# The opening of layer 0 in a two-layer hybrid trunk: another order for loads, sines, angles and rotations

## The chip, the cores and the metric

The kernel runs on one core of a Trainium2 chip. The metric is the device time of one execution in microseconds (us). The core has five instruction queues that run beside each other: TensorE (PE, matmuls and transposes), VectorE (DVE), ScalarE (ACT), GpSimd (POOL) and SyncE (SP, which here only starts DMAs). They meet by semaphores. An instruction that waits holds up everything behind it in its own queue.

## The reference

Two layers over 256 tokens of width 1024, float32. Each layer normalises x, multiplies it with `w_in`, splits the result among three mixers, joins them with `w_out`, and adds a squared-ReLU MLP:

```
h = rms_norm(x, ln1_g[layer])
(a_q, a_ckv, a_kr, i_q, i_k, i_w, b_u, c_q, c_kv, c_gate) = split(h @ w_in[layer])
a_out = dsa_mixer(...)    # an indexer scores keys, top-64 of them are attended to; partial rotary
b_out = s5_mixer(b_u, ...)  # complex diagonal state space, 64 states in 16 groups
c_out = nsa_mixer(c_q, c_kv, c_gate, ...)  # compressed, selected and window branches
x = x + concat(rms_norm(a_out), rms_norm(b_out), rms_norm(c_out)) @ w_out[layer]
x = x + relu(rms_norm(x, ln2_g[layer]) @ w_up[layer])**2 @ w_down[layer]
```

After the second layer x is normalised once more. The rotary angles are `positions * THETA**(-2i/n)`, and the S5 part needs the powers of `exp((lambda_re + i*lambda_im) * exp(log_step))`.

## The kernel before, in words

**Weights in pieces.** All weights go through a ring of four buffers `raw[0..3]` of 128 x 1024 elements. SP loads piece n. ACT rounds it (`hi(n)`, w_hi, line 871). DVE takes the rest of it (`lo(n)`, w_lo, line 1314). PE multiplies in three passes (`mm3`, line 1744): high by high, low by high, high by low. `lo(n)` frees the raw buffer, so it lets SP start piece n+4; PE's last matmul on piece n frees w_hi for `hi(n+4)`. Pieces 0 to 19 are `w_in`, in five column tiles of four pieces each (`TILES`; tiles 0, 2, 3 have 512 columns, tile 1 has 308, tile 4 has 280). Pieces 20 to 31 are `w_out`, the rest `w_up` and `w_down`. The activations are split the same way: `h_parts` (ACT, h_hi, line 864) and `h_rest` (DVE, h_lo, line 1242), from x that PE transposed block by block (`transpose_x`, line 1773; x comes in four column blocks of 256, two blocks of 128 rows of h each).

**The order is written by hand.** Each engine's program is one list; nothing moves at run time. In the opening of layer 0:

- SP (line 496 on) starts `pos_i`, `step_rows` and four small row loads into `vrow_a`, then pieces 0 to 3 (`first_pieces`), then the rows of `vrow_b`, `craw`, the parameters `ukv` and `glw`, then the pieces that wait for `lo`.
- ACT (line 844 on) starts the four x blocks and `braw` (`load_b`). Then it copies the transposed rows (`vectors`), makes h_hi and w_hi in turn, does the S5 sines (`s5_trig(0)`), the rope sines of `ang` and `ang3`, the sums of squares of x (`sums`), the table `ct` (`c_table`), and `hi(4)` on.
- DVE (line 1230 on) does the rope angles (13 small instructions from line 1258 to 1270), clears `tk`, then h_lo and w_lo in turn, `turn()` (which writes the sine and cosine tables from the rope sines), and from `lo(8)` on places other work behind each piece by the table `behind` (line 1599): the six steps `far_...` write `ca`, the six steps `near_...` write `bp`, `index_heads` rotates the indexer's queries and keys, `latent_heads`, `queries` and `keys_s` rotate the others, and behind piece 19 stand `s5_lags`, `s5_sums_read`, `s5_states`, `index_sum`, `s5_states_back`.
- POOL (line 588 on) does `prep(0)` (the S5 angles, which ends in `den_s5`), `prep_powers(0)` (ends in `prep_a`; in the middle it makes `r1` from ACT's sums), `prep_rest(0)` (ends in `prep_b`), starts the compression weights, and `prep_outputs(0)`, which fills `rot` by doubling (`double`, 6 instructions each; ends in `prep_r`) and makes `rkv`.
- PE (line 1736 on): all four x blocks are transposed, then `tile(0)` to `tile(4)`, with other work behind some pieces by the dictionary `after`.

After `tile(4)` come ten units of attention in which PE, DVE, ACT and POOL hand each other scores (line 1638 is the DVE end of it), then `w_out` and the MLP, which are almost all matmuls.

Of the kernel before, what the change touches and what calls it, by code (L numbers as in the profile page):

```python
# [43 lines left out]
CQ = 8  # L44
# [97 lines left out]
def trunk(nc, x_in, positions, ln1_g, w_in, kv_norm_g, w_uk, w_uv, s5_lambda_re, s5_lambda_im,  # L142
# [4 lines left out]
    with ctx:  # L147
# [193 lines left out]
        tk_in = [sig(f"tk_in{i}", 0) for i in range(DEPTH)]  # L341
        ix_roped, a_roped = sig("ix_roped", 1), sig("a_roped", 1)
# [154 lines left out]
        def _(sp):  # L497
            sp.dma_start(pos_i[:], positions.rearrange("o (t p) -> p (o t)", p=PART)).then_inc(pos_loaded.sem, 16)
            sp.dma_start(step_rows, s5_log_step.rearrange("l (j g) -> j l g", g=2)).then_inc(step_row.sem, 16)
            sp.dma_start(vrow_a[0:8], ln1_g.rearrange("l (k p) -> k l p", p=PART)).then_inc(rows_a.sem, 16)  # L500
            sp.dma_start(vrow_a[8:16], s5_lambda_re.rearrange("l (j g) p -> j l (g p)", g=2)).then_inc(rows_a.sem, 16)
            sp.dma_start(vrow_a[16:24], s5_lambda_im.rearrange("l (j g) p -> j l (g p)", g=2)).then_inc(rows_a.sem, 16)
            sp.dma_start(vrow_a[24:32], ln2_g.rearrange("l (k p) -> k l p", p=PART)).then_inc(rows_a.sem, 16)

# [9 lines left out]
            first_pieces(0, lambda q: None)  # L514
# [10 lines left out]
            load_params(sp, 0, params0, ("rows",))  # L525
            for L in range(DEPTH):
# [7 lines left out]
                for c0, w in TILES[1:]:  # L534
                    for q in range(4):
                        piece(n, raw[:, n % RING, 0:2 * w].rearrange("p (k n) -> p k n", k=2),
                              w_l[:, 2 * q:2 * q + 2, c0:c0 + w])
                        n += 1
                wo_l = w_out[L].rearrange("(k p) n -> p k n", p=PART)
                wo_c = w_out[L, D_MODEL - C_HEADS * HD:D_MODEL].rearrange("(g j d) n -> d g j n", g=C_KV, d=HD)  # L540
                for half, _, qs, _ in OUT:
                    for q in qs:
# [9 lines left out]
                        if L == 0 and n == 24:  # L552
                            lags_in(sp, L)
# [34 lines left out]
        def _(pool):  # L588
# [112 lines left out]
            def double(e, n, m):  # L701

                w = [e[:, i, :, n:n + 1].to_broadcast([PART, PAIRS, m]) for i in range(2)]
                return cmul(e[:, 0, :, n + 1:n + 1 + m], e[:, 1, :, n + 1:n + 1 + m], e[:, 0, :, 1:1 + m],
                            e[:, 1, :, 1:1 + m], w[0], w[1],
                            *(t[:, 0:PAIRS * m].rearrange("p (j m) -> p j m", m=m) for t in small))

            def prep_outputs(occ):
# [11 lines left out]
                if occ == 0:  # L720
                    rstd(0, 2, rkv[:], stat[:, 2:4], A_RANK)
# [44 lines left out]
            for L in range(DEPTH):  # L766
# [78 lines left out]
        def _(act):  # L845
# [34 lines left out]
            for b in range(4):  # L880
                cols = slice(b * SEQ, (b + 1) * SEQ)
                act.dma_start(x[:, :, cols], x_in.rearrange("o (t p) d -> p (o t) d", p=PART)[:, :, cols])\
                    .then_inc(x_loaded[b].sem, 16)
            load_b(act, 0, first0)

# [9 lines left out]
            vectors(1, pb[6], 0, 40)  # L895
            act.wait_ge(vec_sb.sem, 1)
            for L in range(DEPTH):
                if L == 0:
                    step_s5.by(act.activation(sp[:, 0, :], lam[2][:, 0], ACT.Exp))
                for n in range(4):  # L900
                    if L == 0:
                        h_parts(L, 0, g1[:, L], (2 * n, 2 * n + 1))
                    hi(L, n)
                    if L == 0 and n == 0:
                        act.wait_ge(lrs_s5.sem, lrs_s5.at(0, 1))
                        mag_s5.by(act.activation(sp[:, 1, :], sp[:, 21, :], ACT.Exp))
                    if L:
                        h_parts(L, 0, g1[:, L], (2 * n, 2 * n + 1))
# [13 lines left out]
                if L == 0:  # L922
                    s5_trig(0)
# [3 lines left out]
                    sums(0, 0, sq_sum.by)  # L927
                    c_table(0, 1)
                for n in range(4, 6):
                    hi(L, n)  # L930
# [31 lines left out]
                act.wait_ge(ix_ps.sem, ix_ps.at(L, 1))  # L962
                step(act.activation(iqT, pb[3][:, 0:SEQ], ACT.Copy), False)
                ix_sb.by(act.activation(ikT, pb[3][:, SEQ:2 * SEQ], ACT.Copy))
# [266 lines left out]
        def _(dve):  # L1231
# [14 lines left out]
            for t, v in ((half_neg, -0.5), (cmask, 0.0), (mask8, 1.0), (mhalf, 1.0), (mquart, 1.0),  # L1246
# [9 lines left out]
            dve.wait_ge(pos_loaded.sem, 16)  # L1256
            dve.wait_ge(freq_set.sem, 1)
            step(dve.tensor_copy(pos_f[:], pos_i[:]))
            nf = HALF + I_HALF
            tt(ang[:], pos_f[:].unsqueeze(2).to_broadcast([PART, TT, nf]),  # L1260
               freq[:].unsqueeze(1).to_broadcast([PART, TT, nf]), ALU.mult)
            ts(ang3[:], ang[:], 1.0 / PI2, MAGIC, ALU.mult, ALU.add)
            ts(ang3[:], ang3[:], -MAGIC, None, ALU.add)
            for c in (C1, C2, C3):
                ts(ang2[:], ang3[:], c, None, ALU.mult)
                tt(ang[:], ang[:], ang2[:], ALU.subtract)
# [1005 lines left out]
```

## Time and profile before

| what | value |
|---|---|
| time, median of 3 runs | 657.12 us (655.36 to 657.30) |
| the profiled execution's own time | 657.18 us |
| its span, first to last instruction | 655.4 us |
| PE busy | 618.9 us, 94% of the span |
| DVE busy | 430.0 us, 66% |
| ACT busy | 361.6 us, 55% |
| POOL busy | 234.6 us, 36% |
| chain that ended last | PE 73%, DVE 15%, ACT 5%, issue 3%, POOL 2%, DMA 1% |
| DMA | 102.79 MB, mean 157 GB/s |

The span is what the trace covers; 1.8 us of the time lie around it. "Chain" is the list of work followed back from the last instruction, at each step to what released it: where it runs through one engine, that engine sets the time there. "Idle before" in a row is how long the engine stood still ahead of an instruction, and what ended it. The matmul rows overlap, so the time that one takes from the next is the distance of their starts.

### The profile page before, as it was taken

Reading aid. Unit: us, or ns where it says so; the run is one execution under the profiler, and the core shown is the slowest. Engines: PE = TensorE matmul, PEld = TensorE weight load, DVE = VectorE, ACT = ScalarE, POOL = GpSimd, SP = SyncE. Lnnn points to the kernel's source line nnn. Section 1 sums busy time; section 2 is a strip of 40 time slices with the busy share of each in tenths; the row PEclk is TensorE's granted clock in tenths of the full one; section 3 lists DMA queues with packets and bytes.
Section 4 is the critical chain, followed back from the end, with each engine's and each line's share of the span. In section 5 each row is a group of like instructions: output and inputs, shape, how many; then the busy total and the mean of one; then the engine's idle time right before and its main releaser. Section 6 shows DMA issues by size and latency. Waiting matters only on the chain.

```text
span 655.4 us, 11268 instructions
## 1 busy us (share of the span) xinstructions
PE 618.9 (94%) x4268; PEld 533.2 (81%) x4268; DVE 430.0 (66%) x796; ACT 361.6 (55%) x674; POOL 234.6 (36%) x407
## 2 busy tenths in 40 slices
PE   5999988998999999999999999799899999999995
PEld 4868865688998899889878787568798899899984
DVE  7599898476655696774575877846755545554553
ACT  5756588735546434443456657984545544444451
POOL 6899258515045999910004304771000000000001
PEclk9999998999999999999999999999899999999998
DMA  9584604156854557366638640314466566657631
GB/s 266 168 235 121 140 2 114 33 155 202 258 186 151 185 164 254 128 226 193 190 83 262 124 129 2 82 65 128 134 216 196 167 200 190 188 166 217 192 98 65
DMA packets 55440, 102.79 MB, mean 157 GB/s; under 512 B 12713, under 2 KB 18906, under 8 KB 55354
## 3 DMA queue, kind: packets, MB, share of 16 engines
q1 hardware_dynamic: 48986, 96.04, 48.2%
q0 software_dynamic: 1792, 4.07, 2.6%
q10 hardware_dynamic: 4608, 1.97, 1.1%
q8 instruction: 34, 0.56, 0.4%
q14 instruction: 20, 0.16, 0.1%
HBM read 99.69 MB, written 1.31 MB: 154 GB/s over the span
## 4 chain that ended last, share of the span: by engine, by line
PE 73%; DVE 15%; ACT 5%; issue 3%; POOL 2%; DMA 1%; SPq 0%; DVEq 0%; POOLq 0%; ACTq 0%
PE pb L1744 72%; DVE w_lo L1314 5%; DVE x L1242 2%; ACT tab_zone L1114 1%; ACT w_hi L871 1%; DVE dtmp L1235 1%; POOL dtmp L794 1%; DVE sc_zone L1638 1%; ACT ptmp L1127 1%; DMA raw<-in_w_in 1%; DVE dtmp L1514 1%; DVE top L1510 1%; PE pb L1871 1%; PE pb L2135 1%; DVE tab_zone L1235 1%
## 5 line engine op out<-in xcount | busy, mean ns | idle before, releaser
L1314 DVE TENSOR_TENSOR w_lo<-raw,w_hi 128x1024 fp32r<-128x1024 f32 (+2 forms) x176 | 223.6, 1286 | 139.5 <-ACT w_hi L871 138.6
L871 ACT ACTIVATE w_hi<-raw 128x1024 fp32r<-128x1024 f32 (+2 forms) x184 | 187.9, 1028 | 201.3 <-PE pb L1744 178.5
L1744 PE MATMUL pb<-h_hi,w_hi 128*128 128x256 f32 x512 | 146.1, 285 | 2.5 <-DVE h_lo L1242 1.8
L1744 PE MATMUL pb<-h_hi,w_lo 128*128 128x256 f32 x512 | 145.6, 284 | 0.0
L1744 PE MATMUL pb<-h_lo,w_hi 128*128 128x256 f32 x512 | 145.5, 284 | 0.0
L1744 PEld LDWEIGHTS pb<-h_hi,w_hi 128*128 128x128 f32 x512 | 98.9, 193 | 4.1 <-DVE w_lo L1314 3.0
L1744 PE MATMUL pb<-w_hi,z_hi 128*128 128x512 f32 x256 | 100.0, 390 | 0.4 <-DVE w_lo L1314 0.4
L1744 PE MATMUL pb<-w_hi,z_lo 128*128 128x512 f32 x256 | 99.9, 390 | 0.0
L1744 PE MATMUL pb<-w_lo,z_hi 128*128 128x512 f32 x256 | 99.7, 389 | 0.0
L1744 PEld LDWEIGHTS pb<-h_hi,w_lo 128*128 128x128 f32 x512 | 99.0, 193 | 0.4
L1744 PEld LDWEIGHTS pb<-h_lo,w_hi 128*128 128x128 f32 x512 | 98.9, 193 | 0.0
L1744 PE MATMUL pb<-w_hi,h_hi 128*128 128x512 f32 (+2 forms) x224 | 85.5, 382 | 4.7 <-DVE w_lo L1314 3.8
L1744 PE MATMUL pb<-w_lo,h_hi 128*128 128x512 f32 (+2 forms) x224 | 82.3, 367 | 0.0
L1744 PE MATMUL pb<-w_hi,h_lo 128*128 128x512 f32 (+2 forms) x224 | 82.2, 367 | 0.0
L603 POOL TENSOR_TENSOR tail<-tail 128x1 f32<-128x1 f32 x2 | 0.4, 194 | 178.6 <-ACT proj L1223 178.6
L794 POOL TENSOR_TENSOR dtmp<-tab_zone,cf 128x128 f32<-128x128 f32 x80 | 38.3, 510 | 62.7 <-DVE cf L1654 60.9
L1744 PEld LDWEIGHTS pb<-w_hi,z_hi 128*128 128x128 f32 x256 | 48.1, 188 | 10.5 <-DVE w_lo L1314 0.9
L1744 PEld LDWEIGHTS pb<-w_lo,z_hi 128*128 128x128 f32 x256 | 48.1, 188 | 10.1
L1744 PEld LDWEIGHTS pb<-w_hi,z_lo 128*128 128x128 f32 x256 | 48.1, 188 | 9.4
L1744 PEld LDWEIGHTS pb<-w_hi,h_hi 128*128 128x128 f32 x224 | 42.6, 190 | 14.4 <-DVE w_lo L1314 6.8
L1744 PEld LDWEIGHTS pb<-w_lo,h_hi 128*128 128x128 f32 x224 | 42.5, 190 | 6.9
L1744 PEld LDWEIGHTS pb<-w_hi,h_lo 128*128 128x128 f32 x224 | 42.7, 191 | 5.9
(309 smaller groups left out, 852.3 us busy)
## 6 DMA issues: line engine op xcount, KB each, us to landing
raw<-in_w_up SPq DMA_DIRECT2D x64, 512.0 KB, 3.7
raw<-in_w_down SPq DMA_DIRECT2D x64, 512.0 KB, 4.2
raw<-in_w_in SPq DMA_DIRECT2D x24, 512.0 KB, 4.9
raw<-in_w_out SPq DMA_DIRECT2D x8, 512.0 KB, 3.7
raw<-in_w_out SPq DMA_DIRECT2D x16, 256.0 KB, 4.1
raw<-in_w_in SPq DMA_DIRECT2D x8, 308.0 KB, 3.2
raw<-in_w_in SPq DMA_DIRECT2D x8, 280.0 KB, 3.0
x<-in_x ACTq DMA_DIRECT2D x4, 256.0 KB, 4.0
```

Of the source, the lines that this page charges most:

```text
L794: w = pool.tensor_tensor(pn[:, i, a:b], ex[:, i, a:b], cf[:, i, t:t + 1].to_broadcast([PART, b - a]), ALU.mult)
L871: hi_made.by(act.activation(w_hi[:, n % RING, 0:width(n)], raw[:, n % RING, 0:width(n)], ACT.Copy))
L1114: w = act.activation(ex[:, i, a:b], sc[:, i, a:b], ACT.Exp, scale=-1.0, bias=nmx[:, i, t:t + 1], accum_out=sm[:, i, t:t + 1])
L1127: w = act.activation(pT[:, 2 * (v % 2) + m, :], pb[2 + m][:, 0:384], ACT.Copy)
L1235: step(dve.tensor_tensor(o, a, b, op), wait)
L1242: return dve.scalar_tensor_tensor(out=o, in0=a, scalar=s, in1=b, op0=op0, op1=op1)
L1314: lo_made.by(dve.tensor_tensor(w_lo[:, n % RING, 0:width(n)], raw[:, n % RING, 0:width(n)], w_hi[:, n % RING, 0:width(n)].bitcast(F32), AL ...
L1510: step(dve.max(top8[:, c:c + 8], isc[:, a:b]), False)
L1514: step(dve.match_replace(isc[:, a:b], top8[:, c:c + 8], isc[:, a:b], -3e38), False)
L1638: w = dve.tensor_tensor_reduce(sc[:, i, a:b], pb[m][:, a:b], mask[:, a:b], -(HD ** -0.5), 3e38, ALU.add, ALU.min, nmx[:, i, t:t + 1])
L1744: return pe.matmul(o, l, r, start=start, stop=stop, skip_group_check=True)
L1871: m = pe.transpose(bank[:, a:a + PART], src[:, t], ident[:])
```

## The change

Only layer 0's opening and its column tiles change (the form of `double` also serves layer 1).

**Loads.** SP no longer starts `pos_i`, `lambda_im` and `ln2_g` ahead of piece 0: the last two go out on ACT's queue behind x's first block, and `pos_i` behind piece 1. `braw` moves from ACT's queue to SP's behind piece 5, and `ukv` and `glw` behind piece 7.

**PE.** Blocks 2 and 3 of x are transposed behind pieces 0 and 1. `index_turned` goes from behind piece 8 to behind piece 10, `index_scores` from behind piece 10 to behind piece 11, `u_transposed` from ahead of piece 12 to behind it.

**ACT.** `hi(0)` stands ahead of the row copy and h_hi; the S5 sines stand between blocks 2 and 3 of h_hi; `hi(4)` stands ahead of the sums, `hi(5)` ahead of `c_table`; the rope sines come after `c_table`. The copy of the turned indexer rows (`index_out`) goes behind `tile_out(1)` and its sums, just ahead of `hi(12)`.

**DVE.** The 13 angle instructions go from the start of the program to behind the last h_lo. The clearing of `tk` goes to POOL, behind `load_c`, with a new semaphore that SP waits for before `lags_in`. `far_re` and `turn()` go behind `lo(7)`. `index_heads` is cut into `index_queries` and `index_keys`, one behind piece 9 and one behind piece 10, and the near and far steps get scratch space of their own.

**POOL.** `double` makes both parts in one instruction where it can, 4 instructions for 6; `rkv` is made behind n = 4 and not behind n = 8.

```diff
+            def load_rows(q):
+                if q == 0:
+                    sp.dma_start(step_rows, ...)
+                    sp.dma_start(vrow_a[0:8], ln1_g...)
+                    sp.dma_start(vrow_a[8:16], s5_lambda_re...)
+                if q == 2:
+                    sp.dma_start(pos_i[:], positions...)
+            first_pieces(0, load_rows)
...
+                        if L == 0 and n == 6:
+                            load_b(sp, 0, first0)
+                        if L == 0 and n == 8:
+                            load_params(sp, 0, params0, ("rows",))
...
+                tt(dst, src, w[0], ALU.mult, False)
+                tt(t, src, w[1], ALU.mult)
+                tt(dst[:, 0], dst[:, 0], t[:, 1], ALU.subtract, False)
+                return pool.tensor_tensor(dst[:, 1], dst[:, 1], t[:, 0], ALU.add)
...
+                    tk_clear.by(pool.memset(tk[:], 0.0))
...
                 if L == 0:
-                    behind = {9: (far_re2, far_re3), 10: (near_re, near_re2), 11: (near_re3, near_im),
-                              12: (near_im2, near_im3), 13: (far_im,), 14: (latent_heads,), 15: (far_im2, far_im3),
-                              16: (queries,), 18: (keys_s,),
+                    behind = {8: (far_re2,), 9: (index_queries,), 10: (index_keys,), 11: (near_re, near_re2),
+                              12: (near_re3, near_im), 13: (near_im2, near_im3), 14: (far_re3, latent_heads),
+                              15: (far_im, far_im2), 16: (queries,), 17: (far_im3,), 18: (keys_s,),
...
+                tile(0, {0: (lambda: transpose_x(0, 0, (2,)),), 1: (lambda: transpose_x(0, 0, (3,)),), 2: (lambda: c_transposed(0),)} if L == 0 else {})
...
-                    tile(2, {0: (index_turned,), 2: (index_scores,)})
-                u_transposed()
+                    tile(2, {2: (index_turned,), 3: (index_scores,)})
```

ACT's queue in the opening, before. `x` is the input, `w_hi<-raw` is hi, `h_hi` comes from x turned into banks pb0 to pb3, `sp<-sp` are S5's exponentials and sines, `ang` the rope sines:

```order
L887 ACTIVATE sp<-half_neg 128x8
L892 ACTIVATE vcol<-pb6 128x2x40
L899 ACTIVATE sp<-vcol 128x8
L864 ACTIVATE h_hi<-pb0,vcol 128x256 x2
L871 ACTIVATE w_hi<-raw 128x1024
L906 ACTIVATE sp<-sp 128x8
L864 ACTIVATE h_hi<-pb1,vcol 128x256 x2
L871 ACTIVATE w_hi<-raw 128x1024
L864 ACTIVATE h_hi<-pb2,vcol 128x256 x2
L871 ACTIVATE w_hi<-raw 128x1024
L864 ACTIVATE h_hi<-pb3,vcol 128x256 x2
L871 ACTIVATE w_hi<-raw 128x1024
```

The same place in the changed kernel, up to the sums of squares:

```order
L882 ACTIVATE w_hi<-raw 128x1024
L904 ACTIVATE vcol<-pb6 128x2x40
L875 ACTIVATE h_hi<-pb0,vcol 128x256 x2
L913 ACTIVATE sp<-vcol 128x8
L875 ACTIVATE h_hi<-pb1,vcol 128x256 x2
L882 ACTIVATE w_hi<-raw 128x1024 x2
L918 ACTIVATE sp<-sp 128x8
L882 ACTIVATE w_hi<-raw 128x1024
L875 ACTIVATE h_hi<-pb2,vcol 128x256 x2
L868 ACT_TABLE_LOAD
L868 ACTIVATE sp<-sp 128x8
L869 ACTIVATE sp<-sp 128x8
```

Piece 0's hi moved ahead of the row copy, of the exponential that POOL waits for, and of the first h_hi; the sines moved ahead of the last pair of h_hi, which is the next row there.

DVE's queue from `far_re` to the end of the indexer's rotation, before. `ca` and `dtmp<-pa,ct` are the far steps, `tab_zone<-pa,bb` is the first near step, `iqr` and `ikr` the indexer's queries and keys:

```order
L1235 TENSOR_TENSOR ca<-pa,ct 128x8x128
L1314 TENSOR_TENSOR w_lo<-raw,w_hi 128x1024
L1454 COPY iqr<-proj 128x256
L1455 COPY ikr<-proj 128x256
L1235 TENSOR_TENSOR dtmp<-proj,ric 128x64
L1235 TENSOR_TENSOR dtmp<-proj,ris 128x8x4 x2
L1235 TENSOR_TENSOR iqr<-dtmp 128x8x8
L1235 TENSOR_TENSOR dtmp<-proj,ric 128x16
L1235 TENSOR_TENSOR dtmp<-proj,ris 128x2x4 x2
L1460 TENSOR_TENSOR ikr<-dtmp 128x8x8
L1239 TENSOR_SCALAR cs<-proj 128x8
L1314 TENSOR_TENSOR w_lo<-raw,w_hi 128x1024
```

The same in the changed kernel, from piece 8 on:

```order
L1347 TENSOR_TENSOR w_lo<-raw,w_hi 128x1024
L1269 TENSOR_TENSOR dtmp<-pa,ct 128x1024
L1347 TENSOR_TENSOR w_lo<-raw,w_hi 128x1024
L1494 COPY iqr<-proj 128x256
L1495 COPY ikr<-proj 128x256
L1269 TENSOR_TENSOR dtmp<-proj,ric 128x64
L1269 TENSOR_TENSOR dtmp<-proj,ris 128x8x4 x2
L1269 TENSOR_TENSOR iqr<-dtmp 128x8x8
L1347 TENSOR_TENSOR w_lo<-raw,w_hi 128x1024
L1269 TENSOR_TENSOR dtmp<-proj,ric 128x16
L1269 TENSOR_TENSOR dtmp<-proj,ris 128x2x4 x2
L1503 TENSOR_TENSOR ikr<-dtmp 128x8x8
```

The rotation stood whole between pieces 8 and 9; now one far step stands there, and the rotation's halves stand behind pieces 9 and 10.

## Rows read from the trace of the kernel before

**Rows 1.** Chain in order of time, 0 to 150 us: start us, us, what.

```profile
3.09 6.17 DMA raw<-in_w_in
9.28 1.07 ACT w_hi L871
10.37 1.24 DVE w_lo L1314
11.65 10.53 PE pb L1744 x36
...
24.32 0.65 DVE w_lo L1314
...
31.49 1.31 DVE w_lo L1314
```

**Rows 2.** Windows, DVE alone: stretch, length, busy (instructions), PEclk, DMA share, GB/s.

```profile
24.30:31.50 7.20, 6.60 (x19) 1.00 0.59 171
31.50:67.20 35.70, 32.83 (x50) 1.00 0.65 184
```

**Rows 3.** Queues, 4.5 to 6 us: packets, MB, share of 16 engines.

```profile
q10 hardware_dynamic: 465, 0.38, 92.3%
q1 hardware_dynamic: 35, 0.01, 2.9%
```

**Rows 4.** Timeline of ACT: start us, us, instruction, idle before.

```profile
7.64 0.24 ACT L892 ACTIVATE vcol<-pb 128x80 f32<-128x80 f32 x1 [1.82 <-PE pb L1757]
...
8.03 0.82 ACT L864 ACTIVATE h_hi<-pb,vcol 128x256 fp32r<-128x256 f32 x2
...
17.45 0.21 ACT L857 ACTIVATE sp<-sp 128x8 f32<-128x8 f32 x1 [0.69 <-POOL sp L641]
...
18.17 1.05 ACT L875 ACTIVATE proj<-x 128x1024 f32<-128x1024 f32 x1
...
22.66 0.89 ACT L914 ACTIVATE ct<-pb 64x128 f32<-64x128 f32 x4 [2.17 <-PE pb L1808]
23.57 2.62 ACT L871 ACTIVATE w_hi<-raw 128x616 fp32r<-128x616 f32 x4
```

**Rows 5.** Timeline of PE, 11 to 23 us.

```profile
16.08 0.39 PE L1744 MATMUL pb<-w_hi,h_lo 128*128 128x512 f32 x1
...
22.02 0.60 PE L1808 MATMUL pb<-ident,craw 128*128 128x128 f32 x4
22.37 0.48 PE L1744 MATMUL pb<-w_hi,h_hi 128*128 128x512 f32 x1
```

**Rows 6.** Timeline of DVE, 4 to 68 us.

```profile
4.23 0.17 DVE L1258 CAST pos_f<-pos_i 128x2 f32<-128x2 int32 x1
...
7.00 0.18 DVE L1270 TENSOR_TENSOR ang<-ang 128x24 f32<-128x24 f32 x1
...
11.52 0.87 DVE L1242 SCALAR_TENSOR_TENSOR h_lo<-pb,vcol,h_hi 128x256 fp32r<-128x256 f32 x2
...
63.75 0.23 DVE L1235 TENSOR_TENSOR dtmp<-proj,rc 128x64 f32<-128x64 f32 x1 [0.20 <-ACT proj L948]
...
65.55 0.74 DVE L1314 TENSOR_TENSOR w_lo<-raw,w_hi 128x560 fp32r<-128x560 f32 x1 [0.94 <-ACT w_hi L871]
67.23 0.39 DVE L1444 COPY ytok<-pb 128x224 f32<-128x224 f32 x1 [0.94 <-PE pb L1744]
```

**Rows 7.** Timeline of POOL: S5's preparation and the doubling.

```profile
8.21 0.21 POOL L628 TENSOR_TENSOR sp<-vcol,sp 128x8 f32<-128x8 f32 x1 [2.46 <-ACT sp L899]
...
43.70 1.06 POOL L603 TENSOR_TENSOR rot<-rot 128x8 f32<-128x8 f32 x1
...
66.53 0.42 POOL L617 TENSOR_TENSOR rot<-rot,yz 128x120 f32<-128x120 f32 x1
```

**Rows 8.** Timeline of PE, 96 to 103 us: one unit's scores, then the next.

```profile
96.44 0.93 PE L1744 MATMUL pb<-u_zone 64*128 64x128 f32 x8
...
101.21 1.52 PE L1744 MATMUL pb<-u_zone 64*128 64x128 f32 x8 [2.23 <-DVE nmx L1638]
```

More of the change, by code:

```diff
@@ L719, in prep_outputs @@
                     step(double(rot, n, n))
-                if occ == 0:
-                    rstd(0, 2, rkv[:], stat[:, 2:4], A_RANK)
+                    if occ == 0 and n == 4:
+                        rstd(0, 2, rkv[:], stat[:, 2:4], A_RANK)
                 prep_r.by(double(rot, 16, 15))
@@ L926, in _ @@
                     act.activation(ang[:], ang3[:], ACT.Sin).then_inc(trig_rope.sem, 1)
[L927 to L930, printed above, removed]
+                else:
+                    for n in range(4, 6):
+                        hi(L, n)
                 if L:
@@ L961, in _, with index_out @@
                         input_rows(act, L, (n - 9,))
[L962 to L964 removed]
+                def index_out():
+                    act.wait_ge(ix_ps.sem, ix_ps.at(L, 1))
+                    step(act.activation(iqT, pb[3][:, 0:SEQ], ACT.Copy), False)
+                    ix_sb.by(act.activation(ikT, pb[3][:, SEQ:2 * SEQ], ACT.Copy))
+                if L:
+                    index_out()
                 tile_out(1)
@@ L1410, in far_im3 @@
                     dve.wait_ge(prep_c.sem, prep_c.at(L, 1))
+                if L == 0:
+                    lo(0)
+                    h_rest(0, g1[:, 0], lambda k: xT_rows(k, 0), first=0, count=4)
+                    for n in range(1, 4):
+                        lo(n)
+                    h_rest(0, g1[:, 0], lambda k: xT_rows(k, 0), first=4, count=2)
+                    den(0)
+                    h_rest(0, g1[:, 0], lambda k: xT_rows(k, 0), first=6, count=2)
+                    angles()
+                else:
+                    for n in range(4):
+                        lo(n)
+                        h_rest(0, g1[:, L], lambda k: xT_rows(k, 0), first=2 * n, count=2)
+                for n in range(4, 6):
+                    lo(n)
+                for n in range(6, 8):
+                    lo(n)
+                if L == 0:
+                    far_re()
+                    turn()
+                    for b in range(4):
+                        dve.wait_ge(x_loaded[b].sem, 16)
+                    dve.memset(cf[:], 0.0).then_inc(x_new.sem, 3)
+                if L == 0:
+                    dve.wait_ge(vec_sb.sem, 2)
+                ts(glb[:, L], glb[:, L], 0.5, None, ALU.mult)
                 def s5_sums_read():
@@ L1608, in _ @@
                     s5_lags()
-                else:
-                    far_re()
-                    lo(8)
-                index_heads()
-                for n in range(9 if L == 0 else 8, 20):
+                    index_queries()
+                    index_keys()
+                for n in range(8, 20):
                     lo(n)
@@ L1762, in ready, with transpose_x @@
                     pe.wait_ge(lo_made.sem, lo_made.at(L, n + 1))
-                def transpose_x(k_new, stage):
-                    for b in range(4):
+                def transpose_x(k_new, stage, blocks=range(4)):
+                    for b in blocks:
                         if L == 0 and stage == 0:
```

142 lines of the change are left out of this document (69 added, 73 removed).

## The prediction

> **What bounds the kernel now.** I read the chain that ended last first: 73% PE, 15% DVE. In order of time [rows 1] it runs: landing of weight piece 0 at 9.26 us, its hi on ACT, its lo on DVE, PE's first product at 11.65, 36 products, then from 24.32 on DVE's lo instructions. The windows [rows 2] show why: from 31.50 to 67.20 DVE is busy 32.83 of 35.70 us, so from tile 1 to the attention units DVE sets the pace and PE, at the end the busiest engine, waits for it. A PE that finishes a piece sooner there gives nothing unless DVE also gets on sooner. So two questions decide: when does DVE's dense stretch begin, and how much of its idle time is closed. The idle time has few places: 0.20 us at 63.75 (for ACT's tile copy), 0.94 at 65.55 (for hi(19)), 0.94 at 67.23 (for PE's s5_kernel) [rows 6], 2.1 us together, of 2.87 in all that [rows 2] allow.
>
> **The landing of piece 0.** From 4.5 to 6 us the queue of x and braw moved 0.38 MB and the queue of the weights 0.01 MB [rows 3], though piece 0 had been issued at 3.09 [rows 1]: transfers are served about in the order of issue, over both queues. In the new order only block 0 and half of the rest of x are ahead of piece 0, say 0.5 MB less. At 0.38 MB in 1.5 us that is 1.95 us, so it lands at 9.28 - 1.95 = 7.3 us. Bounds: 9.3, if the two queues share and all of x still ends ahead of it; 6.3, if all of the 0.75 MB behind block 0 were out of its way. I take 7.3, as the row is one of service in order.
>
> **PE's start.** hi(0) begins at 7.3; lo(0) begins 1.09 later, as 9.28 to 10.37 [rows 1], at 8.4; the first h_lo begins 1.15 behind it (10.37 to 11.52), and a pair takes 0.87 [rows 6]: 10.4. PE starts at 10.45, where it started at 11.65: 1.2 us sooner. Before, PE needed from 11.65 to 16.08 for ten products, 0.44 us apart, at the lower of its two clocks, and 0.23 apart after [rows 1, 5]. I let ten be slow again: piece 0 ends at 10.45 + 4.4 + 0.5 = 15.35. Four transposes put the next matmul 0.35 later (22.02 to 22.37) [rows 5]: block 2 is turned at 15.7, piece 1 ends 2.75 later at 18.45, block 3 is turned at 18.8. The transposes cost PE nothing net: they are the same sixteen, in other places.
>
> The Trainium skill, "TensorE: Matmul & The Clock Gate", Part 1, says that the number of half-rate matmuls at the start varies from run to run of one kernel (6, 11 or 14 in its example). Ten here fits. By it the sum would be 0.8 us less or more either way, at 0.2 us a matmul (an estimate from its counts); I keep ten.
>
> **The sines and the angles.** POOL's preparation starts on an exponential that now stands behind hi(0), the row copy and a pair of h_hi. It started 0.57 behind the copy (7.64 to 8.21) [rows 4, 7]; now 7.3 + 1.07 + 0.57 + 0.82 = 9.75, 1.55 later than before. The sine that waits for its end came at 17.45 [rows 4], so now at 19.0; two sines take 0.4, and only then comes the last h_hi pair, though block 3 is ready at 18.8: 19.4 to 20.2. DVE's last h_lo is done at 20.65 (0.4 behind). PE ends piece 2 at 18.8 + 2.75 + 0.35 = 21.9, so it is not stopped. Here "sines sooner" costs about 0.5 us. Then the angles: from 4.23 to 7.18, 2.95 us [rows 6]. Before they lay where DVE had nothing to do; now they stand ahead of lo(4), in the gap ahead of 24.32. lo(4) starts at 23.65, 0.7 sooner than 24.32 [rows 1]. ACT: hi(4) to 20.85, the sums 2 x 1.15 to 23.1, hi(5) 0.65, ct 0.9, rope sines 0.4, hi(6) 0.65 to 25.7 [rows 4]. DVE would be ready for lo(6) at 25.2, so it stands 0.5. From lo(4) to lo(8) DVE has the same instructions as before, 31.49 - 24.32 = 7.17 us [rows 1]: lo(8) starts at 23.65 + 7.17 + 0.5 = 31.3, 0.2 us sooner. So the whole opening is worth 0.2 us. r1 now waits for the sums, but POOL's prep_a is ready at about 26.3 (19.4 plus the old 8.0 less six instructions at 0.2), when far_re wants it at 26.9; with that cover gone its wait would count fully, up to 1 us. The clearing of tk fell in DVE's wait for hi(0): worth nothing. On POOL it is needed only when the S5 lags go back in, after piece 23: nothing, bounds 0 to 0.5.
>
> **Tiles 1 to 4.** From lo(8) to s5_lags DVE has the same work as before, 67.23 - 31.49 = 35.75 us with 2.1 idle. lo(9) now stands behind one far step (1.25) and not behind 3.3 us of rotation, so each of lo(9) to lo(14) ends 2 to 3.5 us sooner and PE is ahead: I get piece 15 off at about 59.5 instead of 62.35, s5_kernel at 63.9 instead of 67.1. All three waits close: -2.1. One new wait: index_out stands ahead of hi(12) on ACT and needs transposes that PE makes behind piece 10. lo(10) ends at 38.4, the piece takes 2.75, transposes and two copies 1.3, hi(12) 1.05: ready at 43.6, when DVE wants it at 43.2: +0.4. hi(13) is queued behind it and is not needed until 47. Sum: s5_lags starts 0.2 + 2.1 - 0.4 = 1.9 us sooner. From there to 101 us DVE stays nearly dense and ACT and PE follow it, so the 1.9 us go through to the end.
>
> The DMAs that moved: braw is started behind piece 5 (about 13 us, landing before 25 even at its old 11.5 us, wanted near 31), ukv and glw behind piece 7, wanted by the attention units. Their issues delay pieces 6 and 8 by 1 to 1.5 us in SP's queue, which pieces 4 to 8 can stand (they were rounded only from 23.57 on [rows 4]). Cost 0, bounds -0.3 (less small traffic beside pieces 1 to 3) to +0.5. Doubling in 4 instructions: rkv comes some 7 us sooner and prep_r at about 62, before it is asked for at 66. It gives nothing itself, but without it prep_r (66.95 [rows 7]) would hold back what is gained.
>
> The sum against the profiled execution: 657.18 - 1.9 = 655.3; the median of the runs is 657.12, so I say 655.2.
>
> **The rivals.**
> (a) Piece 0 lands no sooner, at 9.3. For: the same bytes of x still move early, and packets of both queues ran side by side after 6 us. Against: [rows 3]. Everything to lo(8) is 2.0 us later than above, 1.8 later than before; of the 2.1 us of waits all close, and the 0.4 stays: 657.1, no change.
> (b) The slow clock in the attention stage goes. At 101.21 eight score matmuls took 1.52 us, at 96.44 the same took 0.93 [rows 8], and the transposes behind them were slow too: about 1.2 us on the chain. It followed a wait of 2.23 us on PE. If the shift puts this wait otherwise, 1.2 more go: 654.0. For: the clock there is fickle. Against: the same short waits stay. The opposite, a second dip, is as possible.
> (c) The tiles' waits do not close, because hi(19) and s5_kernel still come last: only 0.2 us left, 657.0. Against: PE's lead above.
> (d) Slower: POOL. Its doubling took 23.2 us for 30 instructions from 43.70 to 66.95 [rows 7], 0.77 each; the first, of 8 elements, took 1.06, and the last, of 120, took 0.42 [rows 7], so it is not their size that sets it. DVE's instructions of 1024 elements take 1.2 there. If each of the 20 new ones, twice as wide, is held for 1.2 us in a now denser DVE, POOL starts them at 44.4 and ends at 44.4 + 24 + 1.6 for rkv = 70.0. s5_sums_read, with the states and all units behind it, then runs at 70.0 and not at 67.82: +2.2, 659.4. It decides from 0.95 us an instruction. Against: DVE was as dense before, and the mean was 0.77.
> "GPSIMD Engine Reference", Key points, of the Trainium skill says that GpSimd shares its SBUF interfaces with VectorE and contends with instructions that read two SBUF inputs. The trace agrees with the long ones; by it width matters less than count, which is for fewer instructions.
>
> **How the numbers follow.** My forecast 0.42, (a) 0.17, (b) 0.20, (c) 0.13, (d) 0.08. 0.3%, about what a measurement can tell from no change, is 2.0 us, so 655.15 is the line, close to my forecast: half of its chance lies on either side. Faster: 0.21 + 0.19 + 0.05 of the others = 0.45; slower: 0.07, from (d); within: 0.48. The range reaches from a cleared clock dip with a piece 0 at 6.3 (652.9) to late POOL or no gain with some loss (657.9).
>
> **What would show it.** Right: first product near 10.5; the angles between 20.6 and 23.6 and lo(4) right behind them; lo(8) near 31.3; no waits for hi(19) and the kernel; DVE's copy for s5_lags near 65.3. Wrong: a first product near 12; far_re waiting for POOL; a wait of more than 1 us at lo(12); s5_sums_read waiting for rot; or a shift at 67 us that is not found at 101.

## The result, and the profile after

The changed kernel takes 660.21 us in the median of 6 runs (659.51 to 661.9), the kernel before 657.03 in 6 runs beside it (655.36 to 657.55): ratio 1.0060, 95% interval 1.0046 to 1.0075. By the medians it is slower by 3.2 us, by the ratio, which I use below, by 3.9. I had forecast 655.2, with a range up to 657.9. The profiled execution took 659.51 us with a span of 657.6; that of before had 655.4, so 2.2 us of the loss can be looked for in the two traces.

First the answers to [rows 1] and [rows 2]. The chain of waits of the changed kernel from 0 to 150 us (start, us, what):

```profile
1.92 3.73 DMA raw<-in_w_in
5.66 2.24 issue
7.89 1.07 ACT w_hi L882
8.98 1.23 DVE w_lo L1347
...
11.14 4.64 PE pb L1785 x12
...
20.90 1.04 ACT proj L886 x2
21.99 0.94 issue
23.54 0.76 POOL r L752
...
28.35 1.24 DVE ca L1269
```

And the windows, DVE alone:

```profile
24.30:31.50 7.20, 5.68 (x14) 1.00 0.76 244
31.50:67.20 35.70, 33.69 (x53) 1.00 0.58 160
```

hi(0) starts 1.4 us sooner than before and PE's first product 0.5 sooner (11.14 for 11.65), but then the chain leaves PE and goes over ACT's sums to POOL's r1, its doubling and DVE's far_re at 28.35, where it was on PE and DVE in [rows 1]. DVE's timeline shows the places (start, us, instruction, idle before):

```profile
8.98 1.23 DVE L1347 TENSOR_TENSOR w_lo<-raw,w_hi 128x1024 fp32r<-128x1024 f32 x1 [6.13 <-ACT w_hi L882]
...
20.32 0.88 DVE L1276 SCALAR_TENSOR_TENSOR h_lo<-pb,vcol,h_hi 128x256 fp32r<-128x256 f32 x2 [1.42 <-ACT h_hi L875]
...
24.04 1.55 DVE L1347 TENSOR_TENSOR w_lo<-raw,w_hi 128x616 fp32r<-128x616 f32 x2
...
28.35 1.23 DVE L1269 TENSOR_TENSOR ca<-pa,ct 128x1024 f32<-128x1024 f32 x1 [1.07 <-POOL pa L699]
...
32.41 1.23 DVE L1347 TENSOR_TENSOR w_lo<-raw,w_hi 128x1024 fp32r<-128x1024 f32 x1
...
45.36 1.23 DVE L1347 TENSOR_TENSOR w_lo<-raw,w_hi 128x1024 fp32r<-128x1024 f32 x1 [1.02 <-ACT w_hi L882]
...
68.15 0.38 DVE L1484 COPY ytok<-pb 128x224 f32<-128x224 f32 x1
```

lo(8) starts at 32.41, 0.92 later than in [rows 1], and s5_lags' copy at 68.15, again 0.92 later than in [rows 6]. The three waits of [rows 6] are closed to nearly nothing, one of 1.02 us is new, and the stretch is not shorter.

That loss is not the one of the result. By 101 us it is 0.54 (the scores of 101.21 in [rows 8] start at 101.75), and there they take 0.93 and not 1.52: the granted clock is 1.00 in the window 101.39 to 104.80, where it was 0.50 before. At 142 us, where layer 0's output is added to x, the two traces are 0.07 us apart (142.32 and 142.39). The rest is behind it. Windows of both kernels; columns are stretch, length, then busy time and instructions of PE, PEld, DVE, ACT and POOL, granted clock, DMA share, GB/s. Before:

```profile
142.30:200.00 57.70, 55.56 (x388) 51.78 (x388) 35.76 (x39) 30.38 (x41) 16.36 (x29) 1.00 0.66 207
200.00:300.00 100.00, 99.34 (x620) 89.62 (x619) 73.66 (x46) 48.77 (x54) 74.44 (x96) 1.00 0.56 183
```

After:

```profile
142.30:200.00 57.70, 55.56 (x389) 51.78 (x388) 35.68 (x39) 30.38 (x41) 16.35 (x29) 1.00 0.67 206
200.00:300.00 100.00, 97.62 (x609) 88.02 (x608) 71.28 (x47) 48.37 (x53) 70.35 (x80) 1.00 0.54 179
```

From 142 to 200 nothing differs. From 200 to 300, the middle of layer 0's MLP, PE is busy 1.7 us less. Nothing in the diff stands there except POOL's `double`, which prepares layer 1's S5 tables behind the MLP in 80 instructions where it had 96. The two longest entries of PE's waits there, weight loads (PEld) included, after (us in total, times, longest):

```profile
PEld pb L1785 <- issue: 2.9, 3, 2.3
PE pb L1785 <- DVE w_lo L1347: 2.4, 3, 1.9
```

In the trace of before the second row reads 0.5 us in 2 times. What DVE did, after:

```profile
261.29 1.89 DVE L1347 TENSOR_TENSOR w_lo<-raw,w_hi 128x1024 fp32r<-128x1024 f32 x1 [1.49 <-ACT w_hi L882]
264.17 1.90 DVE L1347 TENSOR_TENSOR w_lo<-raw,w_hi 128x1024 fp32r<-128x1024 f32 x1 [0.99 <-ACT w_hi L882]
267.05 1.90 DVE L1347 TENSOR_TENSOR w_lo<-raw,w_hi 128x1024 fp32r<-128x1024 f32 x1 [0.99 <-ACT w_hi L882]
268.87 2.95 DVE L1726 TENSOR_TENSOR proj<-proj 128x1024 f32<-128x1024 f32 x1
272.95 2.23 DVE L1728 TENSOR_TENSOR z_lo<-proj,z_hi 128x1024 fp32r<-128x1024 f32 x1 [1.13 <-ACT z_hi L1234]
275.11 3.41 DVE L1347 TENSOR_TENSOR w_lo<-raw,w_hi 128x1024 fp32r<-128x1024 f32 x1
...
278.66 0.36 PE L1785 MATMUL pb<-h_hi,w_hi 128*128 128x256 f32 x1 [1.90 <-DVE w_lo L1347]
```

And before:

```profile
265.97 1.23 DVE L1314 TENSOR_TENSOR w_lo<-raw,w_hi 128x1024 fp32r<-128x1024 f32 x1 [1.65 <-ACT w_hi L871]
267.12 2.95 DVE L1685 TENSOR_TENSOR proj<-proj 128x1024 f32<-128x1024 f32 x1
271.21 1.75 DVE L1687 TENSOR_TENSOR z_lo<-proj,z_hi 128x1024 fp32r<-128x1024 f32 x1 [1.13 <-ACT z_hi L1200]
```

The same subtraction takes 1.23 us or 1.90, the square 1.2 or 2.95. What lies beside the long ones are POOL's six output products of 1024 elements (`prep_far`). The first and the last of them, after:

```profile
260.15 1.95 POOL L610 TENSOR_TENSOR ca<-pa,ct 128x1024 f32<-128x1024 f32 x1
...
274.06 3.38 POOL L744 TENSOR_TENSOR ca<-ca,yz 128x1024 f32<-128x1024 f32 x1
```

Before, they ran from 263.18 to 281.4. The shorter doubling brought them 3.0 us forward, to 260.15, so that they cover the last three subtractions of a unit, its square and its z_lo, in series. The next unit's first subtraction, at 275.11, stands behind z_lo in DVE's queue and is itself held (3.41 us for 1.23). PE has no piece left by then and stands 1.90 us, until 278.66.

The six near products came forward by 0.5 us, and z_lo of chunk 3 now takes 2.70 us for 1.23. The rows show what the 0.5 us decide. Before, the first product starts 0.19 us behind z_lo, and it is the product that takes longer:

```profile
224.95 1.23 DVE L1687 TENSOR_TENSOR z_lo<-proj,z_hi 128x1024 fp32r<-128x1024 f32 x1 [1.13 <-ACT z_hi L1200]
225.14 2.84 POOL L603 TENSOR_TENSOR tab_zone<-pa,bb 128x1024 f32<-128x1024 f32 x1
```

After, it starts 0.33 us ahead of z_lo, and it is z_lo that takes longer:

```profile
224.63 1.95 POOL L610 TENSOR_TENSOR tab_zone<-pa,bb 128x1024 f32<-128x1024 f32 x1
224.96 2.70 DVE L1728 TENSOR_TENSOR z_lo<-proj,z_hi 128x1024 fp32r<-128x1024 f32 x1 [1.13 <-ACT z_hi L1234]
```

To compare traces whatever lies ahead of the MLP, I take the time between two of DVE's subtractions, the one at 206.57 us in the kernel before and the thirty-sixth behind it, at 303.57: 97.00 us before, 98.7 in the changed kernel (206.66 to 305.38), 1.7 more. Below this is called the MLP stretch.

### The profile page after: what moved, and what is told of

Same layout as the page of the kernel before. It is cut to its first block, busy times and chain, and to the rows that moved or that the text cites. A ratio compares the mean times of both kernels' runs of the same rounds, so it can differ in the third digit from the quotient of the medians.

```text
span 657.6 us, 11239 instructions
## 1 busy us (share of the span) xinstructions
PE 615.7 (94%) x4268; PEld 530.9 (81%) x4268; DVE 429.4 (65%) x795; ACT 361.6 (55%) x674; POOL 226.8 (34%) x376
## 4 chain that ended last, share of the span: by engine, by line
PE 69%; DVE 19%; ACT 4%; issue 4%; POOL 3%; DMA 1%; DVEq 0%; SPq 0%; POOLq 0%; ACTq 0%
PE pb L1785 67%; DVE w_lo L1347 6%; POOL dtmp L805 2%; DVE dtmp L1269 2%; DVE x L1276 2%; DVE sc_zone L1679 1%; ACT w_hi L882 1%; DVE dtmp L1557 1%; PE pb L1912 1%; DVE z_lo L1728 1%; ACT ptmp L1161 1%; DVE top L1553 1%; ACT tab_zone L1148 1%; DVE proj L1726 1%; DVE ca L1269 1%
## 5 line engine op out<-in xcount | busy, mean ns | idle before, releaser
L1347 DVE TENSOR_TENSOR w_lo<-raw,w_hi 128x1024 fp32r<-128x1024 f32 (+2 forms) x176 | 220.5, 1267 | 142.8 <-ACT w_hi L882 142.0
L1785 PEld LDWEIGHTS pb<-w_lo,z_hi 128*128 128x128 f32 x256 | 48.1, 188 | 10.2
```

The lines of the kernel that those rows point to most:

```text
L1347: lo_made.by(dve.tensor_tensor(w_lo[:, n % RING, 0:width(n)], raw[:, n % RING, 0:width(n)], w_hi[:, n % RING, 0:width(n)].bitcast(F32), AL ...
L1785: return pe.matmul(o, l, r, start=start, stop=stop, skip_group_check=True)
```

## The experiments

Theory T: the loss is where POOL's wide products lie against DVE's work at a unit's end. Rival R: it is the opening and its new waits. Each ratio is to the kernel before, run on the same chip, with its 95% interval; 0.1% is 0.66 us. `zlo_sb` counts the z_lo of the MLP's chunks, so value c + 1 is chunk c.

**The old doubling in the changed kernel.**

```diff
-                src, dst = e[:, :, :, 1:1 + m], e[:, :, :, n + 1:n + 1 + m]
...
+                return cmul(e[:, 0, :, n + 1:n + 1 + m], e[:, 1, :, n + 1:n + 1 + m], e[:, 0, :, 1:1 + m],
...
```

The four instructions of the change are six again, in both layers.

> The changed kernel with POOL's old doubling (six instructions of 8 rows) in both layers; all else as changed. Theory T: the new doubling brings POOL's twelve 1024-wide products of layer 1's preparation forward inside layer 0's MLP (8.. by 0.5 us, the six output products by 3.0 us), where they lie on DVE's work at the end of two units; the PE then waits 0.5 us at 240-243 and 1.9 us at 277. With the old doubling the six products start at 263 again and the MLP is as before: 2.0 us sooner than the changed kernel, about 658.2 in the median. Rival R (the opening is what costs, lo(8) is 0.9 us late and far_re waits for POOL): the slower doubling makes far_re later still by 0.5 us, so 660.2 to 660.8.

658.08 us, 1.0012 (0.9998 to 1.0026): 0.48% under the changed kernel, as T says and against R. The size is less sure than the sign: the 12 runs lie in two groups, five at 655.4 to 656.4 and seven at 657.8 to 658.9, and by the medians the gain is 1.6 us. In its trace the MLP stretch is 96.98 us and PE is busy 99.36 us from 200 to 300, both as before, although lo(8) starts at 34.08, the latest of all.

**The new doubling alone, in the kernel before.** The edit is the change's `double` and nothing else.

> The kernel before with the new doubling alone. Theory T: the MLP of layer 0 loses what the changed kernel loses there, 2.0 us: 659.0. Rival R (the loss is in the opening): POOL only finishes sooner, 656.5 to 657.0.

659.19 us, 1.0038 (1.0026 to 1.0050). One function that shortens POOL's work makes the kernel 2.5 us slower, and its PE is busy 97.63 us from 200 to 300, as in the changed kernel. Its MLP stretch is 100.2 us, 3.2 more than before and not 1.7. The other 1.5 us are TensorE's clock: directly behind PE's wait the granted clock is 0.50 for 3.4 us (window, then busy times, granted clock, DMA share, GB/s).

```profile
278.69:282.10 3.41, 3.41 (x18) 3.41 (x17) 2.36 (x3) 0.00 (x0) 0.00 (x0) 0.50 0.89 280
```

In the profiled execution of the changed kernel it is 1.00 at that place; in that of the run with the turn first (below) it is 0.50 from 279.27, and the stretch is 100.2 again. So what the wait costs is 1.7 us in one execution and 3.2 in another.

**The changed kernel with two waits more on POOL.**

```diff
                     prep_rest(L + 1)
+                    pool.wait_ge(zlo_sb.sem, zlo_sb.at(L, 4))
                     prep_near(L + 1)
...
                     pool.wait_ge(prep_r.sem, prep_r.at(L + 1, 1))
+                    pool.wait_ge(zlo_sb.sem, zlo_sb.at(L, 6))
                     prep_far(L + 1)
```

> The changed kernel with two waits more on POOL in layer 0's MLP: the six near products of layer 1's preparation wait for z_lo of chunk 3, the six output products (now at 260 to 277) for z_lo of chunk 5. Each six then lie between two unit ends and not on one. Theory T: the 2.0 us come back and DVE's square and z_lo at 267 to 273 take 1.23 each instead of 2.95 and 2.23: 2.0 to 2.7 us under the changed kernel, 657.5 to 658.2. If contention costs the same wherever the products lie (rival U), 660.2. Rival R: 660.2.

656.77 us, 1.0006 (0.9995 to 1.0017). POOL now waits 10.2 us ahead of the output products, and the kernel is 0.54% faster than the changed one, 3.5 us, more than the 2.0 to 2.7 of theory T. Its MLP stretch is 95.6 us, 3.1 less than in the changed kernel and 1.4 less than before. Its DVE, and its PE from 200 to 300:

```profile
267.03 1.23 DVE L1349 TENSOR_TENSOR w_lo<-raw,w_hi 128x1024 fp32r<-128x1024 f32 x1 [1.65 <-ACT w_hi L884]
268.18 1.22 DVE L1728 TENSOR_TENSOR proj<-proj 128x1024 f32<-128x1024 f32 x1
270.52 1.23 DVE L1730 TENSOR_TENSOR z_lo<-proj,z_hi 128x1024 fp32r<-128x1024 f32 x1 [1.13 <-ACT z_hi L1236]
271.67 6.98 DVE L1349 TENSOR_TENSOR w_lo<-raw,w_hi 128x1024 fp32r<-128x1024 f32 x3
```

```profile
200.00:300.00 100.00, 100.00 (x627) 90.78 (x627) 77.59 (x47) 49.83 (x56) 70.15 (x80) 1.00 0.56 183
```

The contention has not gone: three subtractions now take 6.98 us, 2.33 each. They lie where PE has pieces in stock, as its busy time of 100.00 us shows. So rival U, that it costs the same wherever it lies, falls.

**The second wait alone, in the changed kernel.**

> The changed kernel with the second wait alone (output products behind z_lo of chunk 5); the near products stay at 224.6 on z_lo of chunk 3, which took 2.70 us there. By the profile of the changed kernel the first meeting costs 0.48 us of TensorE and the second 1.9: so 0.5 us more than with both waits, 1.0013 of before, and 2.9 under the changed kernel. If the first meeting costs nothing: 1.0006, as with both.

657.62 us, 1.0020 (1.0009 to 1.0031): 0.40% under the changed kernel, 0.14% above both waits. z_lo of chunk 3 took 2.70 us, and PE waited 0.17 us at 241.49 and 0.30 at 244.93. Its MLP stretch is 96.6 us, 1.0 more than with both waits. So of the 3.1 us between the changed kernel and both waits the near products' meeting is about a third by the traces, and a quarter by the ratios, whose intervals overlap; the output products' meeting is the rest.

**The two waits in the kernel before.**

> The kernel before with the two waits on POOL alone (near products behind z_lo of chunk 3, output products behind z_lo of chunk 5). Theory T (POOL's 1024-wide products on a unit's end hold DVE's square and z_lo, and through them TensorE): before has one such meeting left, at 267 to 273 (square 2.95 instead of 1.22, z_lo 1.75 instead of 1.23) and TensorE 0.66 us idle between 270 and 290, so 0.7 us under the kernel before. Rival U (contention costs the same wherever it lies): no difference. Rival V (the output products are now late, up to 289, and something waits for them): 0.5 to 2 us slower.

654.8 us, 0.9986 (0.9975 to 0.9996). Rival V falls: nothing waits for the late products. The kernel before had one such meeting, and two lines remove it: in the trace the square takes 1.22 us for 2.95 and z_lo 1.23 for 1.75, and the MLP stretch is 95.6 us for 97.0.

**The new doubling and the two waits, in the kernel before.**

> The kernel before with the new doubling and the two waits. Theory T: the new doubling costs nothing by itself, its 2.5 us are all from where it puts the wide products; with the waits their place is fixed and the time is that of before with the waits, 0.7 us under before. Rival W (the wider doubling instructions themselves hold DVE in the opening and at 245 to 260, beyond the place of the products): 0.5 to 2 us more than before with the waits.

655.44 us, 0.9984 (0.9972 to 0.9996). With the products' place fixed the new doubling costs nothing that the runs can tell, and the MLP stretch is 95.6 us here too. T holds and rival W falls.

**The turn of the table ahead of far_re, in the changed kernel.**

```diff
+                    turn()
                     far_re()
-                    turn()
```

> The changed kernel with DVE's turn of the angle table (2.5 us) ahead of far_re, which now waits 1.07 us for POOL's powers at 27.3. The wait is filled and lo(8) starts at 31.35 instead of 32.41. Rival R (the opening sets the loss): 1.0 us under the changed kernel, 659.2. Theory T: the gain of 1 us at lo(8) is there, too, but what reaches the end depends on whether the product stream waits behind it; the 0.9 us lost at lo(8) was seen up to the units at 78 and only 0.07 of it at 142 us, so between 659.2 and 660.2, and the 2.0 us of the MLP stay.

658.9 us, 1.0035 (1.0019 to 1.0051), 0.25% under the changed kernel, whose interval it just overlaps. In its trace lo(8) starts 0.4 us sooner (31.97) and s5_lags' copy 1.0 us sooner (67.17). So this wait was probably a second, smaller loss.

**Both mends in the changed kernel.**

> The changed kernel with both mends: the two waits on POOL and DVE's turn of the angle table ahead of far_re. If the two losses are apart and add, 3.4 + 1.3 us under the changed kernel: ratio to before about 0.9985, 655.5. If they overlap (rival), as with the waits alone: 1.0006, 656.8.

655.22 us, 0.9986 (0.9973 to 1.0000). The two gains add: 0.74% under the changed kernel, and 0.20% under the waits alone, again with intervals that just overlap. But that is only where the kernel before stands with the two waits, so opening and tiles together give nothing that the runs can tell. The next runs take parts from this kernel.

**The tiles' part undone.**

```diff
-                    behind = {8: (far_re2,), 9: (index_queries,), 10: (index_keys,), 11: (near_re, near_re2),
...
+                    behind = {8: (index_queries, index_keys), 9: (far_re2, far_re3), 10: (near_re, near_re2), 11: (near_re3, near_im),
...
-                    tile(2, {2: (index_turned,), 3: (index_scores,)})
+                    tile(2, {0: (index_turned,), 2: (index_scores,)})
+                u_transposed()
...
-                    tile(3, {0: (u_transposed,), 1: (s5_inputs,), 3: (s5_sums,)})
+                    tile(3, {1: (s5_inputs,), 3: (s5_sums,)})
```

On ACT `index_out` stands ahead of `tile_out(1)` again and `u_rows` ahead of hi(14).

> The same with the tiles' part undone: DVE's table of work behind each lo, ACT's transposed index tiles and u rows, and TensorE's transposes in tiles 2 and 3 in the order of before; the opening up to lo(8) stays. My forecast gave that part 1.7 us. If that holds, 1.7 us slower than with it (1.0012 of before). What the traces say (the stretch from lo(8) to s5_lags took 35.74 us in both orders, and 35.2 with the turn first): 0 to 0.5 us slower (0.9986 to 0.9994).

656.14 us, 0.9998 (0.9988 to 1.0009). By the ratios the part is worth 0.12%, about 0.8 us, between the two expectations, but the intervals overlap. In the traces the stretch from lo(8) to s5_lags takes 36.25 us without the part and 35.16 with it, 1.1 us.

**The order of the loads undone.** `pos_i` and all rows go ahead of the weights again, on ACT's queue nothing stands between x's blocks and `braw` comes behind them, and `ukv` and `glw` go behind `craw`.

> The same as with the two waits and the turn first, with the DMA order of before alone: all rows, all of x and braw ahead, so piece 0 lands near 9.3 instead of 7.8, with ACT's hi(0) first in its order. lo(0) is 1.5 us later. If TensorE's start reaches lo(8): 1.5 us slower (1.001 of before). Rival: DVE's pace from lo(4) hangs on the sums, the sines and POOL's powers and not on piece 0; these wait behind hi(0) on ACT as well, so at least 1 us is seen at lo(4), and DVE being full nothing takes it back; 0 only if lo(8) does not move.

655.71 us, 0.9999 (0.9985 to 1.0013), so perhaps 0.13%, with intervals that overlap. lo(0) starts at 10.25 for 8.77 and lo(4) at 26.40 for 24.41 in its trace, but the profiled execution was one of the longer ones (658.75 us), with the granted clock at 0.50 from 86.5 to 93.4 and again from 103.6 to 110.4 us. I take from it that the new order moves piece 0 by about 1.5 us, and no price.

**Layer 0's doubling of the rotation powers left out.**

```diff
-                for n in (1, 2, 4, 8):
+                for n in (1, 2, 4, 8) if occ else (4,):
                     step(double(rot, n, n))
...
-                prep_r.by(double(rot, 16, 15))
+                prep_r.by(double(rot, 16, 15) if occ else double(rot, 1, 1))
```

POOL fills `rot` with a constant first, so this kernel leaves out the rotation powers of layer 0, and its result is not the reference's.

> The changed kernel with the two waits and the turn first, and layer 0's doubling of the rotation powers left out on POOL (16 of 20 instructions; the powers are a constant there, which is wrong data at the same cost elsewhere). Theory S (the 2 us of DVE's idle time that the new order of the tiles closes are given back as longer DVE instructions beside POOL's doubling: DVE was busy 33.9 us of 35.2 between lo(8) and s5_lags, 32.84 of 35.74 before, for the same instructions): DVE's busy time there falls to 32.6 or less and s5_lags comes about 1 us sooner, 0.5 to 1 us under the kernel with the waits and the turn first (0.9986 of before), about 0.9975. Rival (DVE's time there does not hang on POOL's small instructions): no difference.

Of the 20 instructions 12 are left out, not 16 as I had written: four are kept and four stay with one column each. 653.52 us, 0.9958 (0.9945 to 0.9971). DVE alone from lo(8) to s5_lags, first with the doubling and then without it:

```profile
31.58:66.74 35.16, 33.90 (x50) 1.00 0.64 171
```

```profile
32.40:65.83 33.43, 32.16 (x50) 1.00 0.69 187
```

The same 50 DVE instructions are 1.74 us shorter when most of POOL's small instructions are not beside them: POOL's doubling costs DVE's time. s5_lags' copy comes 0.9 us sooner (65.83 for 66.74). How much of that reaches the end is not shown. The ratio is 0.28%, 1.8 us, lower, but the two profiled executions take 653.59 and 653.63 us. The five runs here all have a mean granted clock of 0.994 or 0.995; of the 12 runs with the doubling the five at 0.994 take 653.6 to 654.0, too, and the seven at 0.986 to 0.992 take 655.0 to 656.6. So most of the 0.28% may be the clock.

**The angles moved up, and the angles at the start.** In one kernel `angles()` stands behind the third pair of h_lo; in the other ahead of lo(0), with the load of `pos_i` first.

> The same as the changed kernel with the two waits and the turn first, and DVE's rotation angles (2.9 us) moved up from behind the last h_lo to behind the third pair of h_lo, where DVE waits 0.7 us for POOL and 1.4 us for h_hi. lo(4) could start 1.5 to 2 us sooner, but hi(5) to hi(7) on ACT end at 23.7 and 26.2, so lo(8) moves by 0.3 to 0.6 us: 0.4 us under the kernel with the turn first and the waits. Rival: DVE after 24 us is full and PE is fed anyway, so nothing; or the last h_lo is 0.6 us late and TensorE waits for it, 0.3 us slower.

> The changed kernel with the two waits and the turn first, with DVE's rotation angles back at the start (behind the first clears, ahead of lo(0)) and the positions' load ahead of all. DVE has no work before 8.9 there. If the angles behind the last h_lo (21.1 to 24.1, lo(4) right behind them) are what the opening costs, lo(4) starts near 21.5 and lo(8) about 1 us sooner: 0.9 us less, 0.9972 of before. Rival (then hi(5), at 23.7 behind the sums on ACT, and hi(7) hold DVE just as long): lo(8) within 0.3 us, 0.9986.

655.24 us, 0.9992 (0.9977 to 1.0008), and 657.87 us, 1.0019 (0.9999 to 1.0039). Neither is faster. The first has no trace to read from (its profiled execution took 1723 us). In the second lo(4) does start at once behind the last h_lo, and then DVE waits, as the rival said:

```profile
22.58 0.84 DVE L1348 TENSOR_TENSOR w_lo<-raw,w_hi 128x616 fp32r<-128x616 f32 x1
25.21 0.80 DVE L1348 TENSOR_TENSOR w_lo<-raw,w_hi 128x616 fp32r<-128x616 f32 x1 [1.79 <-ACT w_hi L883]
27.11 1.66 DVE L1348 TENSOR_TENSOR w_lo<-raw,w_hi 128x616 fp32r<-128x616 f32 x2 [1.09 <-ACT w_hi L883]
```

The angles are hidden behind ACT's sums. This kernel is 0.33% slower than the one with both mends. Its opening began later (lo(0) at 9.87 for 8.77), and in most of its runs the clock was lower: four runs with a mean granted clock of 0.994 or 0.995 take 655.1 to 655.5 us, the eight at 0.979 to 0.991 take 657.0 to 662.6. In the profiled one it was down for a long stretch:

```profile
80.00:84.00 4.00, 2.83 (x48) 1.99 (x44) 3.52 (x19) 1.62 (x7) 0.00 (x0) 1.00 0.05 5
84.00:98.00 14.00, 13.28 (x110) 9.37 (x112) 10.56 (x57) 9.86 (x34) 8.00 (x13) 0.54 0.01 1
```

**The tiles' part, the doubling and the waits on the opening of before.**

> The kernel before with the two waits, the new doubling and the tiles' part of the change (DVE's table of work behind each lo, ACT's index_out and u rows, TensorE's transposes in tiles 2 and 3), and the opening up to lo(8) as before. The tiles' part was worth 0.12% in the changed kernel and the kernel before with waits and doubling stands at 0.9984: if they add, 0.9972, 654.5 at a before of 656.35. If the tiles' part needs the new opening's earlier pieces, 0.9984 or a little above.

655.33 us, 0.9981 (0.9967 to 0.9995), beside 0.9984 without the tiles' part, which the runs do not tell apart. In the traces the stretch from lo(8) to s5_lags is 35.2 us with the part and 35.8 without. Four kernels stand at 0.9981 to 0.9986, about 1.1 us under the kernel before and 5 under the changed one, and the runs do not tell them apart. The one to keep is the kernel before with the two waits: two added lines, and the same time.

## Why the prediction was wrong

**The step that failed** is the cost of the new doubling: "It gives nothing itself, but without it prep_r would hold back what is gained." I priced `double` in layer 0's opening, for and against, and in rival (d), and did not ask where else it is called. Layer 1's preparation calls it in layer 0's MLP, ahead of twelve products that the change does not touch. That term was 0 in my sum. The traces show +1.7 us in the MLP stretch of the changed kernel, and +3.2 in the two executions whose clock fell behind the wait; the runs show +2.5 (alone, in the kernel before). The two waits take back 3.5 in the runs and 3.1 in the trace, since they also remove the 1.4 us that the kernel before lost there. My list of what would show me wrong had two signs that came, far_re waiting for POOL and more than 1 us at lo(12), but it looked no further than 101 us.

Between my forecast and the two profiled executions lie 4.1 us (2.2 longer where I had 1.9 shorter): 1.1 from the opening, 1.7 from the tiles, 1.7 from the MLP, 0.4 behind it, less 0.8 that came back between 68 and 142 us. The other steps follow.

**far_re's wait.** I had POOL's powers ready at 26.3 and DVE there at 26.9. They came at 28.3, since r1 waited for the sums until 23.26 and then the doubling of 32 and 64 elements took 0.67 to 0.89 us an instruction beside DVE, where I had subtracted 0.2 for each one saved. I wrote that without cover the wait would count fully, up to 1 us; it was 1.07, and lo(8) started at 32.41 for my 31.3. The turn in front gave back 0.25%, 1.6 us, with overlapping intervals; its trace shows 1.0 us at s5_lags.

**Tiles 1 to 4: -1.7 was expected.** The waits did close as said, and hi(12) was late as said (1.02 for 0.4). But the stretch from lo(8) to s5_lags stayed 35.74 us in both traces, as DVE was busy 33.89 instead of 32.84 with the same work. I had taken DVE's durations as fixed. With the tiles' part undone the kernel is 0.8 us slower by the ratio (intervals overlap) and its stretch 1.1 us longer. The waits and their closing I had right; that the closed time would all be gained I had wrong, and about half of it was.

**The opening** was forecast at 0.2 us, with piece 0 at 7.3: hi(0) came at 7.89, nearer to my figure than to the 9.3 of rival (a), and the first product at 11.14 for 10.45. What the load order is worth the runs do not tell from nothing (0.13%). The sines came at 18.70 and 18.95 for 19.0, the angles at 21.11 for 20.65, lo(4) at 24.04 for 23.65.

**The rivals.** (b) happened in the trace: the slow clock at 101 us is gone there. Of the 0.92 us lost at 68, 0.54 are left at 101 and 0.07 at 142, so about half came back behind the scores, where the clock differed; what gave back the rest is open. The kernels with both waits or the second alone, which have the same opening, have no slow clock at 101 either, but one of 3.4 us from 151 and 152 us on, so the gain is not one to count on. It had a chance of 0.20 and would have led to a gain. (d) named the right resource, POOL's instructions against DVE's, at the wrong place: prep_r was ready at 64.3, 2.6 us sooner than before, and the mean of an instruction was under 1.0. (c) came near the right size for tiles and opening, none, but its reason was wrong: the waits for hi(19) and s5_kernel did close. The upper end of my range, 657.9, lay under my own rival (d), 659.4, so the range left that rival out. The 0.77 us an instruction in (d) also counts the 1.6 us of rkv; without it the mean was 0.72.

## What to carry to other kernels

When a helper is made cheaper, list every place that calls it and look at what its caller does next: here the saving itself was harmless and the products queued behind it moved onto the critical instructions of another engine. On POOL and DVE ask not how much work there is but what it lies beside; long POOL work belongs where DVE's results are in stock, and one wait for a result that ends the critical group holds it there better than the luck of the preceding durations. Compare nearly equal kernels by a stretch of the trace that holds the change, too, and not by their times alone: here executions of one kernel at a different granted clock lay 1 to 3 us apart. Idle time of an engine that others contend with is not free to fill: check whether the neighbours' instructions grew.

## What the runs showed of the hardware

- Beside POOL's products of 1024 elements DVE's subtraction of 1024 elements took 2.97 us in the median of eight, from 227 to 245 us, and 1.23 us alone. The product took 1.95 us where DVE was idle at its start (224.63, 260.15) and 2.93 in between: one DVE instruction for one of POOL, each waiting for the other. That fits an exclusive turn and not a shared rate. Whichever started first had the turn (z_lo and the first near product at 225 us, above). The Trainium skill, "SBUF — State Buffer", Who interferes with whom, says this of a DVE instruction with two SBUF inputs and a GpSimd instruction that reads SBUF. The trace agrees (2.97 for 1.23).
- Small instructions are enough, in both directions: POOL's of 8 to 64 elements took 1.1 to 1.3 us beside DVE's of 1024 and 0.2 to 0.3 alone, and leaving 12 of 20 out took 1.74 us off DVE's busy time.
- The granted clock differed between nearly equal kernels. Of the 15 traces used here, six (the kernel before among them) have 0.50 for 3.4 us between 101 and 106 us, five between 150 and 158, two for longer between 85 and 111 (0.54 over 14 us with the angles at the start), and two have it nowhere from 20 to 200 us. The same wait of 2.2 us stood ahead of the scores at 101 us before and in the changed kernel, and the clock fell in the first alone. Where it fell between 150 and 158, the time from DVE's subtraction at about 144 us to the fourth behind it is 13.9 to 14.0 us and not 12.5. In the runs with both mends a mean granted clock of 0.994 goes with 653.6 to 654.0 us and one of 0.986 to 0.992 with 655.0 to 656.6.
